# Gate and up projections by Strassen's seven products in a two-block fp32 kernel

## The reference

```
def _swiglu(h, w_gate, w_up, w_down):
    return (jax.nn.silu(h @ w_gate) * (h @ w_up)) @ w_down

for layer in range(2):
    x = x + 0.5 * _swiglu(_rmsnorm(x, g[0]), w_gate[layer, 0], w_up[layer, 0], w_down[layer, 0])
    x = x + mixer(_rmsnorm(x, g[1]))      # layer 0: convolution and RWKV ("even"), layer 1: attention ("odd")
    x = x + 0.5 * _swiglu(_rmsnorm(x, g[2]), w_gate[layer, 1], w_up[layer, 1], w_down[layer, 1])
```

## Time and profile before

| | |
|---|---|
| time, median of three runs | 2531.78 us |
| span of the profiled execution | 2532.0 us |
| TensorE busy | 2477.2 us, 98% |
| VectorE, ScalarE, GpSimd busy | 1256.3, 869.2, 1182.0 us |
| DMA | 213.29 MB, mean 84 GB/s |
| feed-forward blocks begin at | 477, 1185, 1556, 2150 us |

### The profile page before, as it was taken

How to read it: one execution, slowest core, us unless ns; L and a number is a source line. 1 busy time by engine, 2 the same in 40 slices (tenths; PEclk the granted TensorE clock), 3 DMA queues, 4 the chain that set the end, 5 groups by cost and what they waited for, 6 DMA issues and landing times.

```text
span 2532.0 us, 36509 instructions
## 1 busy us (share of the span) xinstructions
PE 2477.2 (98%) x14083; PEld 1919.9 (76%) x14083; DVE 1256.3 (50%) x1575; ACT 869.2 (34%) x1177; POOL 1182.0 (47%) x582
## 2 busy tenths in 40 slices
PE   8999999999999999889999999999999999999999
PEld 6676767688888777777888887888887557788887
DVE  6999984543322489664333223333225676433301
ACT  5533353432222335235322223223223344322221
POOL 3799844344444457323444444444444202444443
PEclk9999999899999999999999999999999999999999
DMA  5222223233333332003333333333233211333332
GB/s 147 81 75 76 75 84 100 67 100 91 91 94 91 108 88 71 8 3 98 95 93 91 93 92 89 100 92 99 86 95 95 63 41 59 92 91 91 94 93 79
DMA packets 418658, 213.29 MB, mean 84 GB/s; under 512 B 16805, under 2 KB 416987, under 8 KB 418555
## 3 DMA queue, kind: packets, MB, share of 16 engines
q1 hardware_dynamic: 414475, 209.05, 28.9%
q10 hardware_dynamic: 4080, 2.83, 0.5%
HBM read 209.22 MB, written 2.10 MB: 83 GB/s over the span
## 4 chain that ended last, share of the span: by engine, by line
PE 86%; POOL 6%; DVE 4%; ACT 1%; issue 1%; DMA 0%; ACTq 0%; POOLq 0%; DVEq 0%
PE bank L339 24%; PE bank L336 23%; PE bank L332 23%; POOL w_lo L312 2%; PE bank L1340 2%; PE bank L1343 2%; PE bank L1336 2%; DVE bank L1167 1%; PE bank L2840 1%; PE bank L2211 1%; PE bank L2906 1%; POOL tmp L792 1%; POOL tmp L797 1%; POOL tmp L795 1%; PE bank L2837 1%
## 5 line engine op out<-in xcount | busy, mean ns | idle before, releaser
L312 POOL TENSOR_TENSOR w_lo<-w_raw,w_hi 128x1024 fp32r<-128x1024 f32 (+3 forms) x420 | 983.4, 2342 | 1243.2 <-ACT w_hi L303 1235.5
L303 ACT ACTIVATE w_hi<-w_raw 128x1024 fp32r<-128x1024 f32 (+3 forms) x420 | 425.1, 1012 | 1342.9 <-PE bank L339 1176.3
L332 PE MATMUL bank<-hH,w_hi 128*128 128x512 f32 x1712 | 442.3, 399 | 1.0 <-ACT hH L369 1.0
L336 PE MATMUL bank<-hL,w_hi 128*128 128x512 f32 x1712 | 435.4, 395 | 1.6 <-DVE hL L378 1.6
L339 PE MATMUL bank<-hH,w_lo 128*128 128x512 f32 x1712 | 434.2, 395 | 0.0
L332 PEld LDWEIGHTS bank<-hH,w_hi 128*128 128x128 f32 x1712 | 320.6, 187 | 88.0 <-issue 8.4
L336 PEld LDWEIGHTS bank<-hL,w_hi 128*128 128x128 f32 x1712 | 320.9, 187 | 81.9 <-DVE hL L378 3.8
L339 PEld LDWEIGHTS bank<-hH,w_lo 128*128 128x128 f32 x1712 | 320.9, 187 | 78.3
L530 DVE TENSOR_TENSOR tmp<-bank,R 128x512 f32<-128x512 f32 x88 | 60.8, 691 | 393.5 <-PE bank L339 393.3
L536 DVE TENSOR_TENSOR ffn_aL<-tmp,ffn_aH 128x512 f32 (+1 forms) x88 | 156.4, 1777 | 86.2 <-ACT ffn_aH L499 86.2
L339 PE MATMUL bank<-ffn_aH,w_lo 128*128 128x512 f32 x704 | 179.8, 395 | 0.0
(11 more groups left out here) (513 smaller groups left out, 2724.7 us busy)
## 6 DMA issues: line engine op xcount, KB each, us to landing
w_raw<-in_ffn_w_gate SPq DMA_DIRECT2D x88, 512.0 KB, 3.8
w_raw<-in_ffn_w_up SPq DMA_DIRECT2D x88, 512.0 KB, 3.7
w_raw<-in_ffn_w_down SPq DMA_DIRECT2D x64, 512.0 KB, 3.9
w_raw<-in_w_in SPq DMA_DIRECT2D x48, 512.0 KB, 3.8
w_raw<-in_even_w_in SPq DMA_DIRECT2D x26, 512.0 KB, 3.9
w_raw<-in_ffn_w_down SPq DMA_DIRECT2D x32, 384.0 KB, 3.4
w_raw<-in_w_conv_out SPq DMA_DIRECT2D x8, 512.0 KB, 4.0
w_raw<-in_w_out SPq DMA_DIRECT2D x8, 512.0 KB, 3.9
```

Of the source, the lines that this page charges most:

```text
L303: nc.scalar.activation(w_hi[u % 2][:, 0:K, :], w_raw[u % 4][:, 0:K, :], ACT.Identity).then_inc(w_hi_ready, 1)
L312: nc.gpsimd.tensor_tensor(w_lo[u % 2][:, 0:K, :], w_raw[u % 4][:, 0:K, :], w_hi[u % 2][:, 0:K, :].bitcast(F32), ALU.subtract).then_inc(w_l ...
L332: nc.tensor.matmul(out, H[:, k, :], sH[:, k0 + k, :], start=start and k == 0, stop=False)
L336: nc.tensor.matmul(out, H[:, k, :], sL[:, k0 + k, :], start=False, stop=False)
```

## The change

Gate and up of a hidden tile are computed together as a block matrix product: on the left the 2 x 2 blocks are {gate, up} by {K tiles 0 to 3, K tiles 4 to 7}, on the right {K tiles 0 to 3, 4 to 7} by {rows 0 to 255, rows 256 to 511}. Eight block products (4 tiles of K, 256 columns) would be needed; the Strassen scheme (in Winograd's form) needs seven, with sums of blocks on both sides and of the products.

- **Weights** (`gu_load`, `gu_first_sum`, `gu_sums`, `gu_hi`, `gu_lo`): the four blocks of a hidden tile lie in slots 0, 1, 5, 6 of a buffer of seven slots of 512 columns (three such buffers, loaded by two DMAs of 512 KB each when the unit three before is done). GpSimd makes two slots (3 and 4) in one subtraction of 1024 columns; for the first unit of each half VectorE does that. VectorE makes slots 2 and 5. ScalarE rounds all seven in three parts (2, 3, 2 slots), and VectorE, no longer GpSimd, makes the low parts.
- **Activations** (`state_tile_act`, `state_tile_dve`): seven right-hand blocks per tile k of 0 to 3, from tiles k and k + 4 of x. They replace hH and hL before a feed-forward block. Most of the work comes with tiles 4 to 7.
- **Products** (`gu_unit`, `gu_product`): seven products, each 4 tiles of K by three passes by 256 columns. Some are added in PSUM, others copied out by ScalarE (`copy`, five of 256 columns per unit) and added by VectorE (`first_gate`, `ups`). Only the gate is scaled by R; the missing factor of up is applied to the output of the down projection. Two sets of three banks alternate.
- **Halves**: 11 hidden tiles of gate and up, then the down projection over these 11 tiles for all 8 output tiles (K = 6 and 5, added to x with a factor R), then the other 11 and again the down projection. aH and aL shrink to 11 tiles.
- **Around it**: the weights of a block's first unit are loaded and split before the preceding stage ends; the arenas of the mixers move so that these buffers stay free; several semaphores are shared; `first_two` and an unused option that stopped the kernel early are gone; loops are written out.

The core of the diff, with the calls:

```diff
-        FFN_UNITS, FFN_GROUPS = 2 * FT + 3 * DT, 2 * FT + DT
+        FFN_HALF, FFN_UNITS, FFN_GROUPS = 2 * DT, 4 * DT, 2 * DT
+        DOWN_K = [(0, 6), (6, 5)]
...
+        PRODUCT = {"P1": (0, 0, 0), "P2": (1, 1, 1), "P6": (2, 4, 0), "P5": (3, 3, 2), "P7": (4, 5, 0), "P4": (5, 2, 0), "P3": (6, 6, 2)}
+        PART = ((0, 2), (2, 5), (5, 7))
+        STEADY = ("P1", "P2", "P6", "P5", "P7", "P3", "P4")
+        OPENING = ("P1", "P2", "P5", "P6", "P3", "P7", "P4")
...
+        def gu_load(sp, n):
+            before = same_place(n, 3)
+            if before is not None:
+                sp.wait_ge(gu_done, 7 * (before + 1))
...
+            for first, name in ((0, "ffn_w_gate_2"), (5, "ffn_w_up_2")):
...
+                sp.dma_start(dst, src).then_inc(gu_in[s], 16)
...
+        def gu_first_sum(pool, n):
+            pool.wait_ge(gu_in[in_half(n) % 3], LOADED[n])
+            nc.gpsimd.tensor_tensor(w[:, 3:5, :, :], w[:, 5:7, :, :], w[:, 0:6:5, :, :], ALU.subtract)
...
+        def gu_sums(v, n):
...
+            nc.vector.tensor_tensor(w[:, 2, :, :], w[:, 6, :, :], w[:, 3, :, :], ALU.subtract).then_inc(gu_sum, 1)
+            v.wait_ge(gu_sum, gu_sum_no(n, 2))
+            nc.vector.tensor_tensor(w[:, 5, :, :], w[:, 1, :, :], w[:, 2, :, :], ALU.subtract).then_inc(gu_sum, 1)
...
+        def gu_lo(v_, n, part):
+            v_.wait_ge(gu_sum, gu_sum_no(n, 3))
+            v_.wait_ge(gu_hi_ready, 3 * n + part + 1)
+            nc.vector.tensor_tensor(gu_wl[v % 3][:, b0:b1, :, :], gu_w[v % 3][:, b0:b1, :, :],
+                                    gu_wh[v % 2][:, b0:b1, :, :].bitcast(F32), ALU.subtract).then_inc(gu_lo_ready, 1)
...
+        def state_tile_dve(v, e, j, q):
+            if j < 4:
+                V.tensor_tensor(slot(st_f, k, 5), slot(st_f, k, 0), slot(st_f, k, 3), ALU.subtract).then_inc(st_sum, 1)
+                sum_tile(v, j, q)
+                return
+            V.tensor_tensor(slot(st_f, k, 3), slot(st_f, k, 3), slot(st_f, k, 2), ALU.add).then_inc(st_sum, 1)
...
+            V.tensor_tensor(slot(st_f, k, 4), slot(st_f, k, 3), slot(st_f, k, 0), ALU.subtract).then_inc(st_sum, 1)
...
+            V.tensor_tensor(slot(st_f, k, 6), slot(st_f, k, 1), slot(st_f, k, 4), ALU.subtract).then_inc(st_sum, 1)
...
+            for part in range(2):
+                v.wait_ge(st_hi_ready, 8 * e + 2 * k + part + 1)
+                V.tensor_tensor(st_lo[k][part], st_f[k][part], st_hi[k][part].bitcast(F32), ALU.subtract)
+                if part == 0:
+                    sum_tile(v, j, q)
...
 ffn_act, unit n (v is its number in the half):
+                    copy(n, copies[0])
+                    if n % GU_UNITS == 0:
+                        root_act(act, D, EPS6)
+                    if v:
+                        silu(n - 1)
+                    if v + 1 < GU:
+                        gu_hi(act, n + 1, 0)
...
+                    copy(n, copies[1])
+                    if v:
+                        high(n - 1)
+                    copy(n, copies[2])
+                    if v + 1 < GU:
+                        gu_hi(act, n + 1, 1)
...
+                    copy(n, copies[3])
+                    if v + 1 < GU:
+                        gu_hi(act, n + 1, 2)
+                    copy(n, copies[4])
...
 ffn_dve, unit n:
+                    if v_:
+                        gu_lo(v, n, 2)
+                        scale(n - 1)
+                    if v_ + 1 < GU:
+                        gu_sums(v, n + 1)
+                    if v_:
+                        gated(n - 1)
+                    if v_ + 1 < GU:
+                        gu_lo(v, n + 1, 0)
+                    if n % GU_UNITS == 0:
+                        root_dve(v)
+                    first_gate(n)
+                    if v_:
+                        low(n - 1)
+                    if v_ + 1 < GU:
+                        gu_lo(v, n + 1, 1)
+                    ups(n)
...
+        def gu_unit(pe, n):
+            if n % GU_UNITS == 0:
+                for ks in ((0, 1, 2), (3,)):
+                    for name in order[:3]:
+                        product(name, ks, True)
+                norm_pe(pe)
+                order = order[3:]
+            for name in order:
+                product(name, opening=n % GU_UNITS == 0)
...
 down projection, VectorE:
+                    V.tensor_tensor(b_, b_, R[:, :], ALU.mult).then_inc(dve_step, 1)
+                    v.wait_ge(dve_step, dve_sent(dve_step))
+                    V.scalar_tensor_tensor(xT[:, j, :], b_, 0.5, xT[:, j, :], ALU.mult, ALU.add).then_inc(group_read, 1)
```

More of the change, by code:

```diff
@@ L340, in unit, with square_tile @@
             ins.then_inc(unit_done, 1)
[L343 to L360, removed]
-        norm_no = {"act": 0, "dve": 0, "pe": 0, "act_root": 0, "dve_root": 0}
-        def norm_tile_act(act, gcol, j, x_is, q, e):
-            if j == 0 and e is not None:
-                act.wait_ge(a_lo, FT * (e + 1))
-            act.wait_ge(group_read, x_is)
-            nc.scalar.activation(hH[:, j, :], xT[:, j, :], ACT.Identity,
-                                 scale=par[:, gcol + j:gcol + j + 1]).then_inc(h_hi, 1)
+        norm_no = {"act": 0, "dve": 0, "pe": 0, "act_root": 0, "dve_root": 0}
+        def square_tile(act, j, q):
             if j >= 4:
@@ new lines, in ffn_dve, with gu_product @@
+                x_tile(DT - 1)
+        def gu_product(pe, n, name, ks, opening, last):
+            block, i, which = PRODUCT[name]
+            part = PART_OF[block]
+            out = gu_bank(n, which)[:, 0:HT]
+            H, L = gu_wh[in_half(n) % 2], gu_wl[in_half(n) % 3]
+            e = n // GU_UNITS
+            pe.wait_ge(gu_hi_ready, 3 * n + part + 1)
+            for k in ks:
+                if opening:
+                    pe.wait_ge(st_hi_ready, 8 * e + 2 * k + (1 if i < 3 else 2))
+                nc.tensor.matmul(out, H[:, block, k, :], slot(st_hi, k, i), start=name in OPENS and k == 0, stop=False,
+                                 skip_group_check=True)
+            for k in ks:
+                if opening:
+                    pe.wait_ge(st_lo_ready, 8 * e + 2 * k + (1 if i < 3 else 2))
+                nc.tensor.matmul(out, H[:, block, k, :], slot(st_lo, k, i), start=False, stop=False, skip_group_check=True)
+            pe.wait_ge(gu_lo_ready, 3 * n + part + 1)
+            for k in ks:
+                ins = nc.tensor.matmul(out, L[:, block, k, :], slot(st_hi, k, i), start=False, stop=last and k == 3, skip_group_check=True)
+            if last:
+                ins.then_inc(gu_done, 1)
@@ new lines, in ffn_pe @@
+        def ffn_pe(pe, e):
+            for c in range(2):
+                n0 = GU_UNITS * e + GU * c
+                U = U_F[e] + FFN_HALF * c
+                for v in range(GU):
+                    gu_unit(pe, n0 + v)
+                pe.wait_ge(gu_copied, 5 * (n0 + 9) + 5)
+                pe.wait_ge(gu_gate, GATE0 + n0 + 10)
+                pe.wait_ge(gu_up, 2 * (n0 + 9) + 2)
+                for i in range(FFN_HALF):
+                    k0, K = DOWN_K[i % 2]
+                    unit(pe, U + i, K, aH, aL, k0=k0, start=i % 2 == 0, stop=i % 2 == 1, ready=(a_lo, n0 + k0) if i < 2 else None)
@@ L2360, in even_pe @@
                 ins.then_inc(rw["yi_ps"], 1)
[L2361 removed]
+            unit(pe, U_EO, 6, mixH, mixL, stop=False, ready=(h_lo2, MIX0))
             group_means(1)
```

779 lines of the change are left out of this document (436 added, 343 removed).

## The result

The changed kernel takes 2494.7 us (median of four runs, 2492.9 to 2496.7) against 2531.9 (four runs beside it): a ratio of 0.986, interval 0.984 to 0.987. It is 37 us faster; I had forecast 14. The time lies inside the whole range (2455 to 2590), between the forecast's own range (2495 to 2540, missed by 0.3) and that of rival (1) (2464 to 2488). The sign is right, the size is not.

A forecast was written before the change was run, and what follows sets the result against it. The prediction took the kernel to be bound by TensorE's matmul columns in the feed-forward blocks. From 2532 us it took 92 gained in steady units and added 78 lost in openings: 2518 us, whole range 2455 to 2590.

The forecast's parts named there:

- rival (1): GpSimd's hold falls into VectorE's wait, or openings overlap better: period 9.8 to 9.9 us, 2464 to 2488 us; chance 0.25.
- The period, 10.15 us: Steady gate/up unit: 10.15 us instead of 11.2, taken between 9.8 and 10.2 to 10.5; 88 units gain 92 us.
- GpSimd's hold: Steady units: each GpSimd first sum costs VectorE 2.03 us, lifting its 8.2 us to 10.2, above TensorE's 9.8.
- the proportional price: Gate/up on TensorE: matmul time goes by columns, 0.1167 us for 256 columns, 9.8 us for a unit's 84.
- rival (2): A 0.020 us toll stays with each matmul: 10.64 us on TensorE, period 10.75, kernel 2570 us; chance 0.20.
- The openings, 78 us: Starts of the four feed-forward blocks: together lose about 78 us (55 to 95), summed as 39 + 21.5 + 12 + 6.
- the three S of 21, 13 and 17 us: Blocks 1, 2, 3: time from preceding matmuls' end to last state low part; each loses S - 3.9, together 39 us.
- The clock: Each opening's gap lowers TensorE's granted clock: 3 us for the first dense microseconds at 1.2 GHz, 12 us in all.
- GpSimd's share of the openings: Openings: GpSimd operations hold VectorE about 2 us each time; two first sums cost 4 us, three `w_lo` 6 in block 1.
- Turning to down: nothing: Gate/up to down within a block: last tile's 3.9 us of work hides under the first down unit's 4.2 us.
- loads hidden: Weight loads: two 512 KB transfers per pair land 3.8 us after issue, issued two units ahead, so hidden.
- down 123.2 us: Down projection of a block: the same 528 matmuls, unchanged at 123.2 us.

The follow-up runs named there:

- the split: Kernel before, looped gate/up matmuls issued as two 256-column pieces in block 1 and four of 128 in block 2: 2740.0 us (one run).
- both kernels with doubled sums: First weight sum made twice: by GpSimd on the changed kernel, 2685.9 us; by VectorE on the kernel where VectorE makes it, 2567.1 us.
- the filled kernel: Changed kernel plus 128-column matmuls into an unused bank in TensorE's opening waits of blocks 1 to 3: 2490.7 us against 2495.6 unfilled.
- The kernel without the first sums: Changed kernel, but VectorE makes every unit's first weight sum and GpSimd none: 2482.3 us, ratio to the kernel before 0.980.

## Why the prediction was right in sign and wrong in size

The sum was 92 us gained and 78 lost. By the traces, 88 units at 9.968 instead of 11.2 us gain 108.4. A block of 22 steady units and the down projection would take 342.5 us after (369.6 before); the four blocks take 71.1 us beyond that (7.7 before), so the openings lose 63.4. The mixers lose 6.7.

- **The period, 10.15 us: mis-sized by 0.18, 16 us over 88 units.** The step that failed is the one that put GpSimd's hold on top of VectorE's work and took the result, 10.2, as a bound above TensorE's. VectorE's own work was priced right, 8.0 to 8.1 us in the inner units against 8.2. The hold, 2.03 us from one row, is 1.9 there and 1.6 over the half. Together they are no more than TensorE's own time, and that is 9.97 and not 9.8: the proportional price held within 2 ns (0.1187 and 0.1167), and the toll of rival (2) is refuted twice, in the change and in the split. Taking the hold away altogether left the unit as long. Rival (1) had the better number, with 9.8 to 9.9 a little low. Its reason, that the hold falls into VectorE's wait, holds for the 0.6 us that VectorE waits when GpSimd makes no sum; the rest of the hold fills what VectorE had free beside TensorE's 9.97 us.
- **There was no margin, and that was luck.** VectorE's 90% over the half looked as if a microsecond were free; in the inner units it is busy for 9.93 us of 9.96. The forecast had no reason why the two queues should come out equally long. What more work costs there both kernels with doubled sums show.
- **The openings, 78 us: measured 63.** By terms, from the profiled span: the three S of 21, 13 and 17 us came out at 19.6, 10.3 and 14.6, together 32.8 us of loss where I had 39; block 0's state was complete at 508.1 (forecast 508.6), 20.9 us where I had 21.5. The clock cost 4 us in blocks 1 to 3 where I had 9, and I had 3 more in block 0, where the granted clock was 0.64 in the 2.5 us before 508.48 and 1.00 behind it, with the state complete at 508.1. What is left, 5.7 us for root, table load, R and block 0's clock, is a remainder and was not measured by itself. The clock is the term that failed most in proportion: I charged 3 us to each opening for dense matmuls at 1.2 GHz, and the filled kernel got back 0.8, 1.6 and 1.6 us.
- **GpSimd's share of the openings** was right for the first sums in blocks 0, 1 and 3 (4.2, 4.3 and 3.6 us of hold where I had 4) and wrong in block 2 (1.3). For `w_lo` I charged about 2 us each, 6, 8 and 10 us in blocks 1, 2 and 3, and the trace has 4.8, 2.4 and 6.6; against that VectorE waited longer for ScalarE, 5.8 us in block 2 where I had 1. Two errors cancel there in part. The kernel without the first sums opened 3.2 and 5.0 us sooner in blocks 0 and 1.
- **"Turning to down: nothing", "loads hidden", "down 123.2 us"**: right. The two down halves take 61.6 us each (the last of all 63.4), the transfers land 4.0 and 5.3 us after issue, and TensorE has no wait in the half shown.
- **The mixers were left out**, and cost 5.5 and 1.2 us. This hid a part of the two misses above: without it the kernel would have been 44 us faster, where I had 14. At the turn into the even mixer the eighth matmul now waits 1.93 us for ScalarE's hH where it waited 0.19, probably because the down tile is multiplied by R first; the mixer is 1.2 us late from there, in other runs of the changed kernel 2.7, where I had 0.7 for such an end. A further 1 to 4 us arise in the mixer's stage of 64-column matmuls, in each variant otherwise, one stretch at the lower clock among them. Why is not settled.

With these terms the sum closes: 2532.0 - 108.4 + 63.4 + 6.7 = 2493.7 us, the span. That is bookkeeping and no test, since the openings' 63.4 is what the four blocks take beyond their steady units.

## What to carry to other kernels

Cutting matmuls finer trades columns for loads at no loss only down to where the load is as long as the columns: here 256, with 6 ns to spare. The busy share of a side engine over a whole stage doesn't tell whether it can take more, because the stage's light ends are in it: look at inner iterations by themselves, where 90% was 100% and 88% was 94%, and price one more operation on the chip, as here 1.24 us of work cost 1.08. When GpSimd's operation holds VectorE up, giving the small operation to VectorE (1.22 us) can beat the offload (a hold of 1.6 us, and 2.2 in the openings), and delaying the offload only moves the bill.

## What the hardware showed that I had not expected

- 256 columns with a fresh 128x128 load take 0.118 us and 128 columns 0.112 us, at a granted clock of 1.00. Halving the columns again saves 5%.
- A GpSimd sum under way holds a VectorE operation with two inputs in SBUF, of 256 columns as of 1536: 0.42 us became 2.58, 0.68 became 2.86, 1.76 became 3.19. The Trainium skill (SBUF — State Buffer, section Who interferes with whom) says that a VectorE instruction with two inputs in SBUF contends with a GpSimd one that reads SBUF, and that the order of issue decides which of them blocks; the first two rows agree, with VectorE's start 0.04 and 0.07 us behind GpSimd's and its end 0.28 and 0.55 us behind. The mean over a steady half is lower, 1.6 us: some operations come up when the sum is already under way for a while, as the one at 1424.35.
- The lower clock level cost 4 us in three wait-bound openings, 1 us inside them and 3 in the dense matmuls behind the last wait, and cheap matmuls in the waits gave them back.
